# Opening of a two-layer encoder kernel: one transfer per piece, single tiles first, third unit in quarters, twelve opening matmuls

## The reference, cut to what matters

```
for l in range(DEPTH):                                    # DEPTH = 2
    h = rms_norm(x, ffn1_norm[l])
    x = x + 0.5 * swiglu(h, ffn1_w_gate[l], ffn1_w_up[l], ffn1_w_down[l])   # width 2816
    h = rms_norm(x, mix_norm[l]);  p = h @ w_in[l]
    ...                                                   # attention, HGRN2 and S5 head groups on p
    x = x + mix @ w_out[l]
    h = rms_norm(x, ffn2_norm[l])
    x = x + 0.5 * swiglu(h, ffn2_w_gate[l], ffn2_w_up[l], ffn2_w_down[l])

swiglu(x, w_gate, w_up, w_down) = (silu(x @ w_gate) * (x @ w_up)) @ w_down
rms_norm(x, gain) = x * rsqrt(mean(x * x) + EPS) * gain
```

## Time and profile before

| | us |
|---|---|
| median of three runs | 1032.84 (1032.68 to 1032.97) |
| the profiled execution | 1033.05 |
| its span, first to last instruction | 1031.3 |
| TensorE busy | 1023.4 |
| VectorE busy | 680.3 |
| ScalarE busy | 523.5 |

### The profile page before, as it was taken

How to read it: one execution, slowest core, us unless ns; L and a number is a source line. 1 busy time by engine, 2 the same in 40 slices (tenths; PEclk the granted TensorE clock), 3 DMA queues, 4 the chain that set the end, 5 groups by cost and what they waited for, 6 DMA issues and landing times.

```text
span 1031.3 us, 22763 instructions
## 1 busy us (share of the span) xinstructions
PE 1023.4 (99%) x9714; PEld 1006.2 (98%) x9714; DVE 680.3 (66%) x850; ACT 523.5 (51%) x628; POOL 205.0 (20%) x291
## 2 busy tenths in 40 slices
PE   8999999999999999999999999999999999999998
PEld 7999999999899999999999999999998999999998
DVE  7666656788668555555566665668987667555554
ACT  5645434565587534343475454436456765434341
POOL 0000899800002000000020019996000020000000
PEclk9999999999999999999999999999999999999999
DMA  8746454434325464545555555453442265464541
GB/s 301 269 158 209 164 200 162 162 128 161 124 83 204 164 209 164 202 164 200 176 205 207 181 186 204 163 204 123 153 138 92 92 228 204 164 203 163 203 163 42
DMA packets 26821, 178.44 MB, mean 173 GB/s; under 512 B 3121, under 2 KB 4161, under 8 KB 5761
## 3 DMA queue, kind: packets, MB, share of 16 engines
q1 hardware_dynamic: 25632, 173.03, 47.8%
q10 hardware_dynamic: 1008, 4.05, 1.1%
q0 software_dynamic: 112, 0.40, 0.1%
HBM read 176.42 MB, written 1.05 MB: 172 GB/s over the span
## 4 chain that ended last, share of the span: by engine, by line
PE 96%; DVE 2%; DMA 1%; SPq 0%; ACT 0%; issue 0%; DVEq 0%; ACTq 0%
PE ps L815 30%; PE ps L816 30%; PE ps L817 30%; DMA raw<-stream 1%; PE ps L968 1%; PE ps L1021 1%; PE ps L1086 1%; DVE lo L1228 0%; DVE in_lo L1427 0%; PE ps L1082 0%; SPq L363 0%; PE ps L1043 0%; ACT hi L577 0%; PE ps L1062 0%; PE ps L1031 0%; PE ps L1149 0%
## 5 line engine op out<-in xcount | busy, mean ns | idle before, releaser
L1228 DVE TENSOR_TENSOR lo<-raw,hi 128x2048 fp32r<-128x2048 f32 x130 | 302.7, 2337 | 200.0 <-ACT hi L577 199.9
L815 PE MATMUL ps<-xg_hi,hi 128*128 128x256 f32 x1408 | 399.3, 284 | 2.3 <-DVE lo L1311 1.4
L816 PE MATMUL ps<-xg_lo,hi 128*128 128x256 f32 x1408 | 398.4, 283 | 0.0
L817 PE MATMUL ps<-xg_hi,lo 128*128 128x256 f32 x1408 | 398.4, 283 | 0.0
L577 ACT ACTIVATE hi<-raw 128x2048 fp32r<-128x2048 f32 x130 | 247.1, 1909 | 176.4 <-PE ps L817 170.8
L815 PEld LDWEIGHTS ps<-xg_hi,hi 128*128 128x128 f32 x1408 | 270.3, 192 | 2.9 <-issue 2.8
L816 PEld LDWEIGHTS ps<-xg_lo,hi 128*128 128x128 f32 x1408 | 270.3, 192 | 0.1
L817 PEld LDWEIGHTS ps<-xg_hi,lo 128*128 128x128 f32 x1408 | 270.3, 192 | 0.0
L815 PE MATMUL ps<-act_hi,hi 128*128 128x256 f32 x704 | 199.4, 283 | 0.6 <-DVE act_lo L1266 0.6
L816 PE MATMUL ps<-act_lo,hi 128*128 128x256 f32 x704 | 199.2, 283 | 0.0
L817 PE MATMUL ps<-act_hi,lo 128*128 128x256 f32 x704 | 199.2, 283 | 0.0
(11 more groups left out here) (317 smaller groups left out, 1339.0 us busy)
## 6 DMA issues: line engine op xcount, KB each, us to landing
raw<-stream SPq DMA_DIRECT2D x160, 1024.0 KB, 4.9
par<-params ACTq DMA_DIRECT2D x2, 1463.0 KB, 9.1
raw<-stream SPq DMA_DIRECT2D x8, 256.0 KB, 7.3
rows<-stream SPq DMA_DIRECT2D x2, 1024.0 KB, 6.9
x<-xT ACTq DMA_DIRECT2D x4, 256.0 KB, 6.6
out<-x SPq DMA_DIRECT2D x8, 128.0 KB, 2.0
con<-consts POOLq DMA_DIRECT2D x1, 371.5 KB, 6.6
mask<-masks POOLq DMA_DIRECT2D x1, 20.0 KB, 6.7
```

The source lines that it names most:

```text
L815: pe.matmul(acc, w_hi, a_hi, start=start, stop=False, skip_group_check=True)
L816: pe.matmul(acc, w_hi, a_lo, start=False, stop=False, skip_group_check=True)
L817: return pe.matmul(acc, w_lo, a_hi, start=False, stop=stop, skip_group_check=True)
L1228: v.tensor_tensor(lo[slot][:, :], raw[slot][:, :], hi[slot][:, :].bitcast(F32), ALU.subtract).then_inc(lo_written, 1)
```

## The change

Five things change, all before the first down projection:

- Units 0 and 1 come in five pieces, input tiles 0, 1, 2 to 3, 4 to 5 and 6 to 7 (`FIRST`), and each piece is one transfer for both units, into a `raw` tensor that now holds the three slots side by side. SyncE issues five transfers in place of eight.
- `x` comes in five transfers cut in the same way. ScalarE's queue issues tile 0, the gains and tile 1, then the table load and the tiny activation, then the three pairs. GpSimd waits for piece 3 of the five, where it waited for piece 1 of the four.
- ScalarE, VectorE and TensorE work piece by piece by that list: single tiles twice, then pairs.
- Unit 2 is loaded in four quarters of two input tiles, and split in quarters on ScalarE and VectorE. VectorE now makes all of `lo` of unit 2 before it adds the squares up. TensorE takes the unit input tile by input tile, both column halves in one pass (`third_unit`), and runs `row_sums` in front of the last tile.
- 12 matmuls on zeros in place of 18.

```diff
+FIRST = [(0, 1), (1, 2), (2, 4), (4, 6), (6, 8)]
...
-            for q in range(QUARTERS):
-                for s in range(2):
-                    c = slice(q * 512, (q + 1) * 512)
-                    sp.dma_start(raw[s][:, c], stream[s, :, c]).then_inc(first_loaded[q], 16)
+            for q, (at, end) in enumerate(FIRST):
+                c = slice(at * 256, end * 256)
+                sp.dma_start(raw_all[:, 0:2, c], stream[0:2, :, c].rearrange("u p c -> p u c")
+                             ).then_inc(first_loaded[q], 16)
...
+            for q in range(QUARTERS):
+                c = slice(q * 512, (q + 1) * 512)
+                sp.dma_start(raw[2][:, c], stream[2, :, c]).then_inc(third_loaded[q] if q < QUARTERS - 1 else raw_loaded[2], 16)
...
-            pool.wait_ge(first_loaded[1], 32)
+            pool.wait_ge(first_loaded[3], 16)
...
+            for q, (at, end) in enumerate(FIRST):
+                e.dma_start(x[:, at:end, :], xT[:, at:end, :]).then_inc(x_loaded[q], 16)
+                if q == 0:
+                    e.dma_start(g0[:, :], gain0).then_inc(x_loaded[0], 16)
+                if q == 1:
+                    e.wait_ge(once, 1)
+                    e.activation(ln_ms[:, 0:1], eps[:, :], ACT.Copy)
...
-            split_hi(2, 0, 2)
+            for q in range(QUARTERS):
+                c = slice(q * 512, (q + 1) * 512)
+                if q < QUARTERS - 1:
+                    e.wait_ge(third_loaded[q], 16)
+                else:
+                    e.wait_ge(raw_loaded[2], 16)
+                e.activation(hi[2][:, c], raw[2][:, c], ACT.Copy
+                             ).then_inc(first_hi if q < QUARTERS - 1 else hi_written, 1)
...
+                def third_unit():
+
+                    for k in range(KT):
+                        if k == KT - 2:
+                            pe.wait_ge(lo_written, n0 + 3 + RING)
+                        elif k % 2 == 0:
+                            pe.wait_ge(first_lo, 2 * (len(FIRST) - 1) + k // 2 + 1)
+                        if k == KT - 1:
+                            row_sums(norm, False, 3)
+                        for m in range(2):
+                            w = k * 256 + m * P
+                            last = three(bank(6 + m)[:, 0:T], hi[2][:, w:w + P], lo[2][:, w:w + P],
+                                         xg_hi[:, k, :], xg_lo[:, k, :], k == 0, k == KT - 1)
+                    last.then_inc(units_done, 1)
...
-            for _ in range(18):
+            for _ in range(12):
```

More of the change, by code:

```diff
@@ L121, in sem @@
             return ctx.enter_context(nc.semaphore(name))
-        raw = [sb(f"raw{s}", [P, 2048]) for s in range(RING)]
+        raw_all = sb("raw", [P, RING, 2048])
+        raw = [raw_all[:, s, :] for s in range(RING)]
         x = sb("x", [P, KT, T])
@@ L254, in build @@
         consts_loaded = sem("consts_loaded")
-        x_loaded = [sem(f"x_loaded{q}") for q in range(QUARTERS)]
-        first_loaded = [sem(f"first_loaded{q}") for q in range(QUARTERS)]
+        x_loaded = [sem(f"x_loaded{q}") for q in range(len(FIRST))]
+        first_loaded = [sem(f"first_loaded{q}") for q in range(len(FIRST))]
+        third_loaded = [sem(f"third_loaded{q}") for q in range(QUARTERS - 1)]
         first_hi = sem("first_hi")
@@ L831, in row_sums, with ffn @@
                 last.then_inc(sums_done, 1)
-            def ffn(f, n0, norm, begin):
+            def ffn(f, n0, norm):
                 head = f == 0
@@ L838, in ffn @@
                     pe.wait_ge(xg_lo_ready, f * KT + k + 1)
-                    if k == 0:
-                        pe.wait_ge(lo_written, begin)
-                    if k == 6:
+                    starts = [at for at, end in FIRST]
+                    if k == (starts[-1] if head else 0):
                         pe.wait_ge(lo_written, n0 + 2 + RING)
-                    elif k % 2 == 0:
-                        pe.wait_ge(first_lo, k + 2)
+                    elif head and k in starts:
+                        pe.wait_ge(first_lo, 2 * starts.index(k) + 2)
                     if k == 5 and not head:
@@ L852, in ffn, with gate_up @@
                 last.then_inc(units_done, 2)
-                def gate_up(half, n, slot, b, between=lambda: None):
+                def gate_up(half, n, slot, b):
                     pe.wait_ge(lo_written, n + 1 + RING)
                     for m in range(2):
-                        if m == 1:
-                            between()
                         for k in range(KT):
@@ L869, in step @@
                     pe.wait_ge(gu_read, f * ITERS + i + 1)
-                    gate_up(0, n, 2, 4 + 2 * g, lambda: row_sums(norm, False, 3) if head and first else None)
+                    if head and first:
+                        third_unit()
+                    else:
+                        gate_up(0, n, 2, 4 + 2 * g)
                     gate_up(1, n + 1, 0, 4 + 2 * g)
@@ L1269, in ffn_steps @@
             def ffn_steps(f, n0, norm, ahead, stages={}):
-                split_lo(n0 + 2, 2)
-                if f == 0:
+                if f:
+                    split_lo(n0 + 2, 2)
+                else:
                     first_sums()
@@ L1301, in _ @@
             v.memset(forget_w[:, :], 0.0).then_inc(rows_cleared, 1)
-            for q in range(QUARTERS):
-                for m in (2 * q, 2 * q + 1):
+            for q, (at, end) in enumerate(FIRST):
+                for m in range(at, end):
                     rest_of_x(0, m, g0)
                 for s in range(2):
-                    c = slice(q * 512, (q + 1) * 512)
-                    if q < QUARTERS - 1:
+                    c = slice(at * 256, end * 256)
+                    if end < KT:
                         v.wait_ge(first_hi, 2 * q + s + 1)
@@ L1311, in _ @@
                     v.tensor_tensor(lo[s][:, c], raw[s][:, c], hi[s][:, c].bitcast(F32), ALU.subtract
-                                    ).then_inc(first_lo if q < QUARTERS - 1 else lo_written, 1)
+                                    ).then_inc(first_lo if end < KT else lo_written, 1)
             v.tensor_tensor(rows[:, :, :], x[:, :, :], x[:, :, :], ALU.mult).then_inc(first_squares, 1)
+            for q in range(QUARTERS):
+                c = slice(q * 512, (q + 1) * 512)
+                if q < QUARTERS - 1:
+                    v.wait_ge(first_hi, 2 * (len(FIRST) - 1) + q + 1)
+                else:
+                    v.wait_ge(hi_written, 3 + RING)
+                v.tensor_tensor(lo[2][:, c], raw[2][:, c], hi[2][:, c].bitcast(F32), ALU.subtract
+                                ).then_inc(first_lo if q < QUARTERS - 1 else lo_written, 1)
             v.wait_ge(consts_loaded, 32)
```

22 lines of the change are left out of this document (9 added, 13 removed).

## The result

The changed kernel took 1034.08 us, the median of 20 runs (1033.29 to 1035.18), against 1032.70 of before in 20 runs beside it (1032.28 to 1033.36). The ratio is 1.0013 with an interval of 1.0008 to 1.0019, so it is slower by 1.4 us. The prediction was 1032.5 in a range of 1031.2 to 1033.6. The time is outside the range, and on the other side of before than the sum.

The account below looks back on a forecast made before the run. It took TensorE, busy 99% of the span, to bound the kernel. Of 1.5 us gained before the down projection, a 1.2 us wait for `act_lo` left 0.4, rounded to -0.3: 1032.5 us, range 1031.2 to 1033.6.

Parts of the forecast that it names:

- when input tiles 2 and 3 are ready for TensorE: In the opening: `x` lands at 8.2, ScalarE's and VectorE's splits follow, and TensorE gets tile 2 at 11.07 us.
- rival 2: `x` served behind weights issued earlier, landing at 12.2; down projection 2.4 us late, 1035.2 us; chance 0.06.
- the queues share: Argument against rival 2: `x` landings 2.25 us apart with both queues full, 116 of the 311 GB/s.
- ScalarE ready at 5.5: ScalarE's start in the opening, limited by its own queue's issues: 5.5 us, against 5.68 before.
- First matmul 7.45: First real matmul starts 1.95 us behind ScalarE, at 7.45, bounds 7.2 to 7.8; a gain of 1.1 us.
- A stall of 0.7 us before tile 2: TensorE wants tile 2 at 10.33, gets it at 11.07, and stands 0.7 us.
- The clock gap: TensorE idles 1.4 to 2.2 us behind twelve opening matmuls; costed at nothing, bound 1.0 us if its clock halves.
- No standstill before unit 2: The 1.0 us standstill in front of unit 2 goes, and it starts at 19.7 in place of 21.18.
- TensorE waits 1.2 us for `act_lo`: At the first down projection: TensorE arrives at 31.7, `act_lo` allows 32.9, 9.64 us behind `hi` of unit 4.
- Unit 4 lands at 23.3: Unit 4's weights, issued 0.4 us earlier because the last pair's first `lo` starts at 13.94 in place of 14.38.
- rival 3: Small pieces move at 250 GB/s in place of 311, delaying 3.1 MB by 2.5 us: 1035.0 us; chance 0.03.
- the sum of -0.4: Net effect in the profiled execution, between -0.8 and +0.1 us, rounded to -0.3; chance 0.62.

Follow-up runs that it names:

- `x` put back: Changed kernel with `x` again in four transfers of two tiles, the first ahead of the gains, all ahead of the table load: 1032.79 us.
- the shortened chain: Norm's activations moved ahead of `hi` of unit 4, squares and `row_sums` earlier: 1031.96 us on before with unit 2 quartered, 1031.51 with `x` put back, 1032.87 on changed kernel.
- the cut opening: Programs ended once units 0 and 1 are computed, then storing `x`: before 26.86 us, changed kernel 27.72, with `x` put back 26.78.
- the third unit alone: Kernel before with only unit 2 loaded, split and computed in quarters: 1032.89 us, ratio 1.0002.
- the last set of short programs: Programs ended at VectorE's last split of units 0 and 1, TensorE doing two tiles only: before 23.22 us, changed kernel 24.31, with `x` put back 22.55.

## Why the prediction was wrong

**The step that failed is when input tiles 2 and 3 are ready for TensorE, 11.07 us. The prediction took it from `x` alone, landing at 8.2, and put the landing of their weights at nothing.** In the profiled execution `x` landed at 9.17 and tile 2 started at 12.09; in the other profiles of this opening ScalarE got this `x` at 8.70 to 9.80. With `x` put back the same `x` was there by 7.6, but then the weights landed at 9.98, and tile 2 started at 12.11. So in the profiles it is the two transfers together that come 1 us later than the sum had it. In the medians the changed transfers of `x` cost another 1.1 us (1033.93 against 1032.79). Of that the profiles of this pair show nothing; those with the shortened chain, where `x` came as late as 9.80, show 0.76 us of it.

The prediction had the case as rival 2, "Later `x`", and gave it 0.06, with a point of decision at 9.8 (9.7 by its own figures). It argued against it with before's landings 2.25 us apart, "so the queues share". The queues do share, but by then SyncE had issued more bytes. The changed kernel's page gives the groups of transfers (count, KB each, median us to landing):

```profile
raw<-stream SPq DMA_DIRECT2D x3, 512.0 KB, 8.5
...
x<-xT ACTq DMA_DIRECT2D x3, 256.0 KB, 7.9
```

Of before the worst `x` took 8.6 us and the least, its first pair, 4.5. In the changed kernel the first pair is the fourth issue of ScalarE's queue, at 2.24. SyncE's five issues, half a microsecond apart from 0.76, carry 256 KB twice and then 512 KB, so three of them with 1 MB are ahead of it. Before, the same tiles' `x` was issued at 1.69, behind two transfers of weights with 0.5 MB and a third of 0.25 MB that was issued in the same hundredth. At the 337 GB/s that the stretch from 4 to 9 us shows in the changed kernel (the columns of the earlier trace rows),

```profile
4.00:9.00 5.00, 5.00 (x25) 4.30 (x25) 2.26 (x6) 2.23 (x6) 0.00 (x0) 1.00 0.98 337
```

0.25 to 0.5 MB more is 0.8 to 1.6 us, an estimate. Landing in about the order of issue of both queues together fits this: these 256 KB of `x` landed by 7.9 in before (the work on them starts at 7.93) and at 9.17 now, 1.3 later. It is an inference from landings; no run changed the bytes ahead of `x` alone. The Trainium skill (DMA: Bandwidth & Descriptors, the section Queues, rings and completion order) has each DMA engine take turns between the queues, packet by packet. The trace doesn't fit equal turns by bytes: 0.5 MB of `x` had landed by 9.17, and 1 MB of weights by 7.4. The page speaks of packets and not of bytes, so this doesn't decide its rule.

The other steps, in the prediction's order:

- ScalarE ready at 5.5: it was 4.55. I put the issue of the three pairs behind the table load. The queue issued them during it, from 2.24, and the table load started 1.5 us earlier than before. The size was off by 0.95 us, for the good.
- First matmul 7.45, bounds 7.2 to 7.8: 6.76, outside the bounds by the same error. By the prediction's own pitch, 4.55 and 1.95 give 6.50; the opening matmuls held TensorE until 6.76, since the twelve took 5.3 us, about 0.44 each, where I had their end at "5.3, or near 5.8".
- A stall of 0.7 us before tile 2: 2.2 by the view, 2.4 by the starts. 0.7 of the difference is the earlier start, the rest the late `x`.
- The clock gap, costed at nothing with a bound of 1.0: in whole kernels it is not seen in the median (twelve opening matmuls in before: 0.0 us). The longer standstill behind tile 1 does let the clock fall in some executions, as the cut opening showed; it isn't what the median shows, since the 16 runs with a mean clock of 1.000 have a median of 1034.01.
- No standstill before unit 2, "19.7 in place of 21.18": right that it goes; it starts at 20.79. The row sums follow at 25.83 for 24.7, 1.1 us later than my sum like everything behind tile 2 (12.09 for 11.07).
- TensorE waits 1.2 us for `act_lo`: right in kind and place, 0.8 us in size, and 0.78 with the third unit alone. The 9.64 us from `hi` of unit 4 held to the hundredth.
- Unit 4 lands at 23.3: 24.0. It follows the last split, 14.38 in the earlier trace rows and 14.65 after, though the sum had 13.94. This is how the late `x` reaches the end.
- The view of stretches says nothing for small transfers being slow (rival 3): 337 GB/s against 311 in the earlier trace rows.

So the sum of -0.4 had the structure that the profiles show, and one input wrong by 1 us in them, by an estimated 2 in the median, if the 1.1 us above come in at the same place (not shown). The structure made it matter: on the gain's side everything above 0.4 us was already given back to the chain behind unit 4, so an early start could not pay for a late `x`. I costed the late case at 2.4 us, but found its point of decision from TensorE's own work alone. The last split and unit 4 follow the pair directly, so a landing at 9.2 already makes the sum positive. The reason that rival 2 gave, bytes that SyncE has issued first, fits the landings above, and 0.06 was too little for it.

**What stays open.** Why the changed transfers of `x` cost about a microsecond more in most executions than in the profiled ones, and whether `x` or something beside it is then what lands late, no trace shows. A test left undone is the changed kernel with only the three pairs of `x` moved ahead of the table load. Nor is it clear why the opening with `x` put back, 0.67 us faster than before's in the last set of short programs, gives 0.05 us in the whole kernel and 0.45 with the shortened chain.

## What to carry to other kernels

Where two queues fill the memory path from the first microsecond, cost the landing of a piece by all the bytes issued ahead of it on both queues, and for all the transfers that the piece needs: here, with merged weights and one more transfer ahead of it, an input found 0.25 to 0.5 MB more in front, and moving the input forward moved the weights back. Starting 1.8 us earlier gave nothing against that. Before costing an earlier start, follow the chain that the end of the opening hangs on (here the norm behind unit 4's landing) and shorten that first; it was worth 0.9 to 1.3 us in each of three openings. And where the profiled execution is at the edge of the timed ones, cut the stretch out as a kernel of its own and time that, and look first in its profile at what its last instruction waits for, since that is what is timed.

## What the runs showed of the hardware

- A profiled execution can hide a loss: the changed kernel's took 1033.29, the least of 20 with a median of 1034.08; the last of its short programs 23.08, the least of six with a median of 24.31.
- ScalarE's queue issues transfers while a table load that stands ahead of them in the program runs: issues from 2.24 to 3.67, the load from 2.18 to 3.46.
- Twelve or eighteen opening matmuls made no difference that the intervals tell apart (1032.85 and 1032.84 in before, 1033.93 and 1034.20 in the changed kernel), and matmuls of zeros in a standstill of 2 us gave nothing (1033.87).
- Behind a standstill of 2.2 us TensorE went to its lower clock level for 3.2 us in one execution of the cut opening (0.21 us for each matmul of 256 columns) and not in the whole kernel's profile (0.12), whose opening is the same.
- A stretch of 3.3 us at the lower level reads as a mean clock of 0.998 over the whole kernel, so the mean tells runs with such a stretch from others: 16 of the changed kernel's 20 read 1.000, with a median of 1034.01 in place of 1034.08.
- Two transfers that one piece needs traded places: `x` issued at 2.24 landed at 9.17 with its weights at 7.4, and issued at 1.71 it was there by 7.6 with its weights at 9.98.
